# Key products in two banks of their own, and each weight split ahead of the ropes and ada steps

## The reference

```python
h_ctx = modulate(rms_norm(ctx_s, g_mix_pre[layer]), csh_a, csc_a)     # 256 context tokens
s_f, s_b = context_states(h_ctx, w_in[layer], lg_f, lg_b)             # k^T (decay) v over the context
h_lat = modulate(rms_norm(x, g_mix_pre[layer]), sh_a, sc_a)           # 512 tokens
proj = h_lat @ w_in
q, k, v, g, f = jnp.split(proj, [RET_W, 2 * RET_W, 3 * RET_W, 4 * RET_W], axis=-1)
q = apply_rope(q, *rope); k = apply_rope(k * RET_HEAD_DIM ** -0.5, *rope)
o_f = retention_scan(q, k, v, lg_f, s_f, strict=False)                # and backwards with s_b
```

## Time and profile before

| what | value |
|---|---|
| median of three runs | 1497.24 us |
| profiled execution, its own time | 1496.4 us |
| its span in the trace | 1494.6 us |
| TensorE busy | 1414.0 us, 95% |
| VectorE busy | 883.7 us, 59% |
| ScalarE busy | 518.4 us, 35% |
| mean granted TensorE clock | 0.962 |

### The profile page before, as it was taken

How to read it: one execution, slowest core, us unless ns; L and a number is a source line. 1 busy time by engine, 2 the same in 40 slices (tenths; PEclk the granted TensorE clock), 3 DMA queues, 4 the chain that set the end, 5 groups by cost and what they waited for, 6 DMA issues and landing times.

```text
span 1494.6 us, 15947 instructions
## 1 busy us (share of the span) xinstructions
PE 1414.0 (95%) x6412; PEld 1134.9 (76%) x6412; DVE 883.7 (59%) x1047; ACT 518.4 (35%) x667; POOL 26.7 (2%) x23
## 2 busy tenths in 40 slices
PE   5899999969999999997999999999979999999995
PEld 2688688848888888884789887668848888888884
DVE  4776765766776767656789873567464332332334
ACT  4542334243434342222321224573333222323211
POOL 0000000010000000001000000000010000000001
PEclk8999999979999999998999998799989999999998
DMA  9334043504343435563442221002302223232321
GB/s 397 126 113 139 2 155 127 182 16 155 127 165 131 152 144 183 213 224 112 143 146 102 96 86 55 1 1 85 113 28 89 108 84 112 84 109 88 113 85 57
DMA packets 31165, 173.70 MB, mean 116 GB/s; under 512 B 3584, under 2 KB 3840, under 8 KB 15616
## 3 DMA queue, kind: packets, MB, share of 16 engines
q1 hardware_dynamic: 31104, 172.85, 32.0%
HBM read 170.74 MB, written 2.10 MB: 116 GB/s over the span
## 4 chain that ended last, share of the span: by engine, by line
PE 90%; DVE 5%; ACT 3%; issue 1%; DMA 1%; SPq 0%; DVEq 0%; ACTq 0%
PE bank L1182 28%; PE bank L1183 27%; PE bank L1184 27%; PE bank L1430 2%; PE bank L1582 1%; DVE xT L985 1%; DVE yT L984 1%; PE bank L1351 1%; PE bank L1568 1%; PE bank L1569 1%; DMA adaf<-ada 1%; PE bank L1557 1%; DVE tmp L748 0%; ACT rstd L358 0%; ACT WH L348 0%
## 5 line engine op out<-in xcount | busy, mean ns | idle before, releaser
L1182 PE MATMUL bank<-hH,WH 128*128 128x512 f32 x1088 | 432.3, 397 | 20.0 <-DVE hL L753 13.2
L1183 PE MATMUL bank<-hL,WH 128*128 128x512 f32 x1088 | 427.9, 393 | 0.0
L1184 PE MATMUL bank<-hH,WL 128*128 128x512 f32 x1088 | 427.6, 393 | 0.0
L707 DVE TENSOR_TENSOR WL<-raw,WH 128x2048 fp32r<-128x2048 f32 x109 | 249.5, 2289 | 166.6 <-ACT WH L348 166.6
L1182 PEld LDWEIGHTS bank<-hH,WH 128*128 128x128 f32 x1088 | 207.2, 190 | 70.1 <-issue 18.4
L348 ACT ACTIVATE WH<-raw 128x2048 fp32r<-128x2048 f32 x109 | 208.0, 1908 | 147.9 <-PE bank L1184 147.8
L1184 PEld LDWEIGHTS bank<-hH,WL 128*128 128x128 f32 x1088 | 207.0, 190 | 44.1
L1183 PEld LDWEIGHTS bank<-hL,WH 128*128 128x128 f32 x1088 | 207.3, 191 | 43.3 <-issue 1.0
L1182 PE MATMUL bank<-GH,WH 128*128 128x512 f32 x352 | 137.2, 390 | 0.0
L1184 PE MATMUL bank<-GH,WL 128*128 128x512 f32 x352 | 137.0, 389 | 0.0
L1183 PE MATMUL bank<-GL,WH 128*128 128x512 f32 x352 | 136.9, 389 | 0.0
(11 more groups left out here) (259 smaller groups left out, 1848.9 us busy)
## 6 DMA issues: line engine op xcount, KB each, us to landing
raw<-weights SPq DMA_DIRECT2D x110, 1024.0 KB, 4.8
ada_half<-ada_later SPq DMA_DIRECT2D x80, 512.0 KB, 4.6
adaf<-ada SPq DMA_DIRECT2D x8, 1024.0 KB, 17.6
xT<-x_t SPq DMA_DIRECT2D x2, 1024.0 KB, 6.3
out_t<-xT SPq DMA_DIRECT2D x8, 256.0 KB, 2.0
ctxT<-ctx_t SPq DMA_DIRECT2D x1, 1024.0 KB, 27.9
ropeT<-rope SPq DMA_DIRECT2D x1, 512.0 KB, 27.0
bandT<-band SPq DMA_DIRECT2D x1, 448.0 KB, 20.1
```

The source lines that it names most:

```text
L707: TT_(WL[:, slot, :], raw[:, slot, :], WH[:, slot, :], sub).then_inc(s.lo_done, 1)
L1182: mm(o, lh, rh, start=start, stop=False, skip_group_check=skip)
L1183: mm(o, lh, rl, start=False, stop=False, skip_group_check=skip)
L1184: return mm(o, ll, rh, start=False, stop=stop, skip_group_check=skip)
```

## The change

Three things are different.

- The key products of both passes go to banks 6 and 7. In pass 0 they wait for no reader, in pass 1 for the key sums of pass 0. The value products, still in banks 0 and 1, wait for the query sums in pass 0 and for the value copies of pass 0 in pass 1.
- The splits move on ScalarE and VectorE. Chunk 2 is split ahead of the ropes of queries 0 and 1, chunk 3 ahead of those of queries 2 and 3. In the loop chunk 4 + 2p is split right behind the key ropes, ahead of the context keys and the ada steps.
- The attention loop no longer waits for v_read 4 at its start; it does at i = 1 behind the states product, together with a wait for all key sums.

```diff
 # ScalarE; the same moves on VectorE with split_lo
+            split_hi(2, 0)
             for n in range(2):
                 rope_tile(n, bank[n], qH, n, done(C_Q, n, 2), s.q_swap, s.q_sum, s.q_hi)
-            split_hi(2, 0)
...
             norm_hi(0, tmpc, hcH, LC, s.cnorm_mul, s.hc_hi, lambda k: mod0[:, k, 1:2])
+            split_hi(3, 1)
             for n in range(2):
                 rope_tile(2 + n, bank[2 + n], qH, 2 + n, done(C_Q + 1, n, 2), s.q_swap, s.q_sum, s.q_hi)
...
             for p in range(2):
-                split_hi(C_KV + 2 * p + 1, 1)
+                if p:
+                    split_hi(C_KV + 2 * p + 1, 1)
                 for n in range(2):
-                    rope_tile(2 * p + n, bank[n], kH, 2 * p + n, done(C_KV + 2 * p, n, 4), s.k_swap, s.k_sum, s.k_hi)
+                    rope_tile(2 * p + n, bank[6 + n], kH, 2 * p + n, done(C_KV + 2 * p, n, 4), s.k_swap, s.k_sum, s.k_hi)
+                split_hi(C_KV + 2 * p + 2, 0)
                 if p:
                     states_hi(0)
                 for tt in range(TC):
...
-                split_hi(C_KV + 2 * p + 2, 0)
                 if p:
                     decays(0)
...
 # TensorE
                     if p:
-                        pe.wait_ge(s.v_read, n + 1)
-                    else:
-                        pe.wait_ge(s.q_sum, n + 1)
-                    project(bank[n][:, :], slot, n, hH, hL, ALL).then_inc(s.mm_done, step(n, 4))
+                        pe.wait_ge(s.k_sum, n + 1)
+                    project(bank[6 + n][:, :], slot, n, hH, hL, ALL).then_inc(s.mm_done, step(n, 4))
...
-                    if b < 2:
-                        pe.wait_ge(s.k_sum, 2 * p + b + 1)
+                    if b < 2 and p:
+                        pe.wait_ge(s.v_read, b + 1)
+                    elif b < 2:
+                        pe.wait_ge(s.q_sum, b + 1)
...
             pe.wait_ge(s.kc_lo, 4)
-            pe.wait_ge(s.v_read, 4)
...
                 if i == 1:
                     pe.wait_ge(s.state_lo, 1)
                     states(1)
+                    pe.wait_ge(s.v_read, 4)
+                    pe.wait_ge(s.k_sum, HEADS)
```

More of the change, by code:

```diff
@@ L819, in states_lo @@
                     sH[:, :, 2 * p:2 * p + 2, :], sub).then_inc(s.state_lo, 1)
+            split_lo(2, 0)
             for n in range(2):
                 rope_tile(n, bank[n], qH, qL, n, done(C_Q, n, 2), s.q_swap, s.q_sum, s.q_hi, s.q_lo)
-            split_lo(2, 0)
             dve.wait_ge(s.lg_ln, 1)
@@ L830, in _ @@
                     s.cnorm_mul, s.hc_hi, s.hc_lo, crstd)
+            split_lo(3, 1)
             for n in range(2):
@@ L839, in _ @@
             for p in range(2):
-                split_lo(C_KV + 2 * p + 1, 1)
+                if p:
+                    split_lo(C_KV + 2 * p + 1, 1)
                 for n in range(2):
-                    rope_tile(2 * p + n, bank[n], kH, kL, 2 * p + n, done(C_KV + 2 * p, n, 4), s.k_swap, s.k_sum,
+                    rope_tile(2 * p + n, bank[6 + n], kH, kL, 2 * p + n, done(C_KV + 2 * p, n, 4), s.k_swap, s.k_sum,
                               s.k_hi, s.k_lo)
+                split_lo(C_KV + 2 * p + 2, 0)
                 if p:
@@ L862, in _ @@
                     decay_args(0)
-                split_lo(C_KV + 2 * p + 2, 0)
                 for n in range(2):
```

## The result

| | before | after |
|---|---|---|
| median of six executions | 1496.47 us | 1503.14 us |
| lowest to highest | 1493.33 to 1502.03 | 1502.41 to 1505.38 |
| profiled execution (its span) | 1496.4 (1494.6) | 1503.37 (1501.6) |
| mean granted TensorE clock | 0.962 | 0.958 |

What follows compares the result with a forecast made beforehand. TensorE, 90% of the chain, was taken as the bound through idle and half-speed time. An 11.8 us front lead mostly died in VectorE's ada queue, leaving 0.2 to 1.6 gained, middle 0.9: 1496.3 us against the median, range 1491.5 to 1500.5.

Steps and rivals of the forecast that it cites:

- first gap: TensorE idle from 107.5 us, waiting for vc_lo ahead of the first states product at 110.9; 3.4 us.
- second gap: TensorE idle after the first two scores, by 140 us, until vc_lo (2) and the second states product at 147.2; over 7 us.
- The front gaps: TensorE idle at 61.5 to 66.4 and 86.0 to 88.4 us; both go with their slow stretches, TensorE leads by 11.8 us.
- the 3.03 gap: TensorE's old gap at 144 to 147 us, model for the restart near 110.9: 3.4 us at half clock, 1.7 lost.
- The cold stretch: Half clock at the second states product near 147 us; all of it runs cold, costing 1.0 to 2.0 us.
- both kernels have the same chain: Behind the second states product, state copies and cross products run alike; waits for k_sum and v_read cost nothing.
- the unknown of the loads: Three ada loads in a row (steps 3, 7, 9): chain 1.7 us shorter at 3.4 each, 8.4 longer at 6.9 each.
- (c): Rival: slow ada loads on VectorE's way to vc_lo; 1504.7 us at 6.9 each, 1501.4 at 5.8 each; chance 0.08.
- (a): Rival: TensorE's lead gets through, attention loop starts 13 us earlier if ada steps weren't ahead of vc_lo; 1484 us; chance 0.05.
- (b): Rival: part of the lead gets through, loads 3.4 us, clock holds at 110 us; 4.3 gained, 1492.9 us; chance 0.10.
- (d): Rival: split 2 comes early but TensorE still stops at 61.5 us; 1497 us; chance 0.01.
- the two cases at 110 us: Half clock or held clock behind the gap before the first states product; 0.2 or 1.6 us gained in sum, 1.4 apart.

Runs made afterwards that it cites:

- fill_narrow: Kernel after plus 28 and 72 spare 128-column matmuls ahead of TensorE's two waits for vc_lo; 1494.03 us, ratio to before 0.9980.
- ada_late: Kernel after with chunk 6's split back behind the context keys, ada steps 6 to 9 among the Fourier projections, earlier ada steps off vc_lo's way; 1482.22 us, ratio 0.9891.
- fill_wide: Kernel after plus 14 and 36 spare 512-column matmuls ahead of TensorE's two waits for vc_lo; 1492.49 us, ratio to before 0.9975.
- front_only: Kernel after with both loop splits (chunks 4 and 6) back in place, early splits 2 and 3 and banks kept; 1494.98 us, ratio to before 0.9976.
- ctx_first: Kernel after, but in pass 1 TensorE multiplies the context keys ahead of the first states product, behind the same vc_lo wait; 1499.89 us, ratio to before 1.0019.
- split6_back: Kernel after with the split of chunk 6 put back behind the context keys in pass 1; 1492.92 us, ratio to before 0.9968.
- vread_back: Kernel after with the wait for v_read 4 put back at the attention loop's start, ahead of the scores; 1500.22 us, ratio to before 1.0018.
- fill_first_gap: Kernel after plus 28 spare 128-column matmuls in its first gap (107.5 to 111.3 us) only; 1498.69 us, ratio to before 1.0006.
- fill_second_gap: Kernel after plus 72 spare 128-column matmuls in its second gap (142.6 to 151.3 us) only; 1496.73 us, ratio to before 1.0000.

## Why the prediction was wrong

It put 1496.3 (1491.5 to 1500.5) and 0.82 on no measurable change; the time was 1503.14. The steps, as predicted and as found in after:

| step | predicted | measured |
|---|---|---|
| split 2 starts on ScalarE | 54.2 | 54.02 |
| context product starts | 72.5 | 72.18 |
| chunk 3 ends | 95.7 | 95.37 |
| key products end | 107.5 | 107.5 |
| ada step 3 / first states product starts | 108.4 / 111 | 108.70 / 111.33 |
| first gap | 3.4 | 3.79 |
| **half clock behind it** | **3.4 long, 1.7 lost** | **9.0 long, 4.5 lost** |
| chunk 4 done | 121.0 | 124.1 |
| ada step 4 | 130.8 | 134.01 |
| from there to vc_lo | 16.4 | 17.3 |
| second gap | over 7 | 8.54 |
| second states product | 147.2, 5.3 long | 151.31, 5.35 long |
| **half clock past its end** | **none** | **4.4 more, 2.2 lost** |

The path of waits was right to the end. The front gaps went, TensorE led by 11.8 us, and the lead ran into VectorE's list, at the places named. The step that failed is a term of the sum: "as behind the 3.03 gap the next 3.4 us run at half clock, 1.7 lost". It was 9.0 us and 4.5 lost. The time that TensorE itself loses by it vanishes in the second gap; it counts through the split of chunk 6, which waits for chunk 4 and drags step 4 and vc_lo with it: of the 4.1 us by which the second states product is late, 2.8 are this. The same misjudgement stands in "The cold stretch costs 1.0 (if it is only 3.4 us long) to 2.0" and in "Behind it both kernels have the same chain [...] cost nothing": the stretch went on into scores and the cross products, 4.4 us past the product, 2.2 lost. 2.8 and 2.2 are 5.0 of the some 7 us between forecast and result; 0.9 more is the second chain from step 4 to vc_lo, 0.7 is the half weight that the sum gave to a clock that held at 110 us, and the rest is small differences of start. fill_narrow is the test of it: with the clock held, the same order gives 3.0 us less than before.

How it could have been seen: the rows had slow stretches of 5.6, 5.2, 3.4 and 3.7 us, and I took the shortest, for its gap was nearest in length, and the longest of the rows as the cap. Behind the 3.03 gap the row has 3.7 us at 0.55, and 3.4 belongs to the gap of 2.33; the loss is 1.7 us by either, so this slip cost nothing. Nor did two others: step 2 at 106.2 takes 4.0 us for a load and not the 4.8 that the text names, and 129.4 for step 4 with the clock held should be 129.2. The range carried the unknown of the loads (up to 8.4 us) and nearly none for the clock. The same trace held longer ones that the rows leave out, one of 30.7 us (0.50 over 922.2 to 952.9) and, among others, this one of 10.2 us:

```profile
21.10:31.30 10.20, 9.54 (x52) 5.49 (x49) 4.17 (x9) 2.65 (x6) 0.00 (x0) 0.50 1.01 426
```

Four rows of 3.4 to 5.6 were no ground for a bound, the more so where the product behind the gap (24 matmuls of 128 columns) was one that no row showed at a restart.

Of the rivals, (c), slow loads, gave a time near the one measured, 1504.7, but by luck and for another reason: the loads that its chain hangs on took 3.4 (step 2), 5.2 (step 3), 4.6 (step 7) and 3.5 us (step 9), a mean of 4.4 for the three in its sum, the very point from which it was to turn to a loss and no more. The Trainium skill (DMA: Bandwidth & Descriptors, Latency and other measured facts), by which a load was estimated at 3.2 us, is near two of the four (3.4 and 3.5) and too low for the other two. (a), the lead gets through, did not happen in after but its condition is what ada_late sets up: take the ada steps from in front of vc_lo, and the time is 1482.22, against the 1484 of that rival. (b) and (d) are not borne out.

The rule of the Trainium skill (TensorE: Matmul & The Clock Gate, What's actually happening) that the gate runs free of the kernel was cited for the two cases at 110 us. A gap of 1.23 us with a slow stretch behind it in fill_wide would fit that. The spread of its executions (1488.8 to 1498.4) shows nothing, for that of the kernel before beside it is nearly as wide (1493.4 to 1502.2). In after, six executions lie within 3 us, so here chance is not what made the loss.

## What to carry to other kernels

A lead that an engine gains is worth nothing until its next wait on a list written out by hand: follow it there, and move what has loads in it from in front of that wait first (here ada_late, 16.3 us), before work is pulled ahead elsewhere. Do not put a split that waits for the engine's own newest product ahead of something the engine wants soon. And a gap costs more than its idle time: before pricing the restart, look up every slow stretch of the trace and not only the one whose gap is nearest in length, leave room above, and follow it past the instruction it begins with.

## What the hardware showed that was not expected

- Most slow stretches behind a gap were 8.2 to 11.4 us long in this part of after and its variants, with gaps of 2.68 to 9.08 us; the earlier trace rows had none over 5.6. Gap and length don't go together: 6.88 us gave 3.5 (front_only), 4.52 gave 4.6 (ctx_first), 4.10 gave 8.6 (split6_back), 3.79 gave 9.0 (after), 2.68 gave 10.1 (vread_back).
- The clock need not fall where the gap ends. In after it fell inside both gaps, 1.3 and 3.7 us ahead of the states products. Behind short gaps it stayed at 1.00 for some 2 us of work and fell then: behind 2.38 us in split6_back (1.00 over 146.9 to 149.0, 0.50 over 149.1 to 152.4), behind 2.26 us in front_only (1.00 over 147.4 to 149.7, 0.50 over 149.8 to 153.1).
- The same happened behind 1.23 us (fill_wide, 0.50 over 113.2 to 119.9) and 0.61 us (fill_first_gap, 0.50 over 112.5 to 119.3), while 0.98 us ahead of chunk 4 and 0.51 ahead of the second states product in fill_second_gap left the clock at 1.00.
- Spare matmuls of 128 columns, 72 of them in a row, held the clock at 1.00 where it already was (fill_narrow, 142.0 to 147.6).
